# Hybrid retention and attention block: the first value projection as one paired group with seven block products, its heads moved into the second retention iteration

## The reference, cut to what matters

```python
xn = rmsnorm(h, norm_w[l], NORM_EPS)
proj = xn @ w_in[l]
(rq, rk, rv, rz, dq, dk, dv, dz, g_ret, g_diff) = jnp.split(proj, SPLIT_POINTS, axis=-1)
rq = apply_rotary(rq.reshape(b, s, RET_HEADS, RET_QK_DIM), ret_cos, ret_sin)
rk = apply_rotary(rk.reshape(b, s, RET_HEADS, RET_QK_DIM) * (RET_QK_DIM ** -0.5), ret_cos, ret_sin)
o_ret = retention(rq, rk, rv).astype(h.dtype)
o_ret = rmsnorm(o_ret, None, NORM_EPS).reshape(b, s, RET_WIDTH) * jax.nn.silu(rz)
```

## Time and profile before

| what | us |
|---|---|
| three runs | 1080.72, 1080.82, 1082.44 |
| their median | 1080.82 |
| the profiled execution | 1081.12 |
| its span, first to last instruction | 1079.3 |
| PE busy | 1070.8 |
| DVE busy | 801.3 |
| ACT busy | 557.4 |

### The profile page before, as it was taken

How to read it: one execution, slowest core, us unless ns; L and a number is a source line. 1 busy time by engine, 2 the same in 40 slices (tenths; PEclk the granted TensorE clock), 3 DMA queues, 4 the chain that set the end, 5 groups by cost and what they waited for, 6 DMA issues and landing times.

```text
span 1079.3 us, 13314 instructions
## 1 busy us (share of the span) xinstructions
PE 1070.8 (99%) x4840; PEld 891.4 (83%) x4840; DVE 801.3 (74%) x1000; ACT 557.4 (52%) x713; POOL 55.6 (5%) x89
## 2 busy tenths in 40 slices
PE   9999999999999999999999999999999999999997
PEld 7888888888888888888888888888888888888885
DVE  6685576766888978867768686787869875677886
ACT  6554454545646544434644654464465554445554
POOL 0100000000000000000100020010002000111100
PEclk9999999999999999999999999999999999999999
DMA  9887666766665565667576667767766667675763
GB/s 327 303 255 213 192 190 197 242 177 194 184 222 181 193 230 176 211 189 241 166 223 203 205 200 201 237 180 208 209 202 184 217 204 243 234 235 186 263 216 117
DMA packets 122209, 227.98 MB, mean 211 GB/s; under 512 B 14496, under 2 KB 36768, under 8 KB 121632
## 3 DMA queue, kind: packets, MB, share of 16 engines
q1 hardware_dynamic: 120832, 224.76, 66.8%
q0 software_dynamic: 1024, 2.10, 0.5%
q10 hardware_dynamic: 288, 0.27, 0.1%
HBM read 210.84 MB, written 2.10 MB: 197 GB/s over the span
## 4 chain that ended last, share of the span: by engine, by line
PE 97%; DVE 1%; DMA 1%; issue 0%; ACT 0%; DVEq 0%; POOLq 0%; POOL 0%; SPq 0%; ACTq 0%
PE bank L1637 21%; PE bank L1639 21%; PE bank L1638 21%; PE bank L1644 10%; PE bank L1646 10%; PE bank L1645 10%; PE bank L1716 1%; PE bank L1715 1%; PE bank L1714 1%; PE bank L1609 0%; DMA raw<-w_out_dram 0%; PE bank L1613 0%; PE bank L1616 0%; PE bank L1770 0%; PE bank L1730 0%
## 5 line engine op out<-in xcount | busy, mean ns | idle before, releaser
L1145 DVE TENSOR_TENSOR w_lo<-raw,w_hi 128x1024 fp32r<-128x1024 f32 x348 | 426.8, 1236 | 220.9 <-ACT w_hi L798 220.0
L798 ACT ACTIVATE w_hi<-raw 128x1024 fp32r<-128x1024 f32 x348 | 367.0, 1059 | 422.8 <-PE bank L1639 316.1
L1637 PE MATMUL bank<-w_hi,xt_hi 128*128 128x512 f32 x880 | 344.0, 391 | 0.0
L1639 PE MATMUL bank<-w_hi,xt_lo 128*128 128x512 f32 x880 | 342.9, 390 | 0.0
L1638 PE MATMUL bank<-w_lo,xt_hi 128*128 128x512 f32 x880 | 342.8, 390 | 0.0
L1639 PEld LDWEIGHTS bank<-w_hi,xt_lo 128*128 128x128 f32 x880 | 165.3, 188 | 34.6
L1638 PEld LDWEIGHTS bank<-w_lo,xt_hi 128*128 128x128 f32 x880 | 165.4, 188 | 33.7
L1637 PEld LDWEIGHTS bank<-w_hi,xt_hi 128*128 128x128 f32 x880 | 165.3, 188 | 33.6
L1644 PE MATMUL bank<-w_hi,xt_hi 128*128 128x512 f32 x312 | 121.6, 390 | 0.0
L1646 PE MATMUL bank<-w_hi,xt_lo 128*128 128x512 f32 x312 | 121.5, 390 | 0.0
L1645 PE MATMUL bank<-w_lo,xt_hi 128*128 128x512 f32 x312 | 121.5, 389 | 0.0
(11 more groups left out here) (209 smaller groups left out, 1061.3 us busy)
## 6 DMA issues: line engine op xcount, KB each, us to landing
raw<-w_in_dram SPq DMA_DIRECT2D x284, 512.0 KB, 4.3
raw<-w_ret_up_dram SPq DMA_DIRECT2D x32, 512.0 KB, 4.7
raw<-w_diff_up_dram SPq DMA_DIRECT2D x32, 512.0 KB, 4.5
raw<-w_out_dram SPq DMA_DIRECT2D x32, 512.0 KB, 4.5
rot<-squares_t SPq DMA_DIRECT2D x64, 64.0 KB, 2.3
zs<-squares_t SPq DMA_DIRECT2D x48, 64.0 KB, 2.3
normed<-squares_t SPq DMA_DIRECT2D x48, 64.0 KB, 2.2
raw<-w_in_dram SPq DMA_DIRECT2D x8, 256.0 KB, 5.5
```

Source lines behind the costliest of these rows:

```text
L798: act.activation(w_hi[:, s, :, :], raw[:, s, :, :], ACT.Copy).then_inc(hi_ready, 1)
L1145: dve.tensor_tensor(w_lo[:, s, :, :], raw[:, s, :, :], w_hi[:, s, :, :].bitcast(F32), ALU.subtract) \
L1637: pe.matmul(bank[bk][:, :], hi, w_hi[:, s, kk, :], start=k == 0, stop=False)
L1639: return pe.matmul(bank[bk][:, :], lo, w_hi[:, s, kk, :], start=False, stop=k == KT - 1)
```

## The change

The two value groups of the first iteration become a fifth paired phase, `VALUES`, of one group: 16 units of 1024 columns on banks 4 to 7 (own) and 0 to 3 (shared), with seven products at its two places. The values are no longer read from banks but from the joined sums in a row of `gate` (`read_value`, `rest_of_value`), after the group's end. So the first iteration's products of scores by values move from behind units 43 and 50 to behind units 50 and 54, beside the second iteration, and with them everything that follows of these heads. The second iteration's rotation of queries moves from steps 13, 14 to 15, 16. The lambda sums move from step 43 to 38.

```diff
-PAIRED = (U_RET_GATE, U_UP, U_DIFF_GATE, U_OUT)
-PAIRED_FIRST = (G_RET, 0, G_DIFF, 0)
+U_VALUES = U_RET + 4 * UNITS
+PAIRED = (U_VALUES, U_RET_GATE, U_UP, U_DIFF_GATE, U_OUT)
+PAIRED_FIRST = (RV, G_RET, 0, G_DIFF, 0)
...
-SUMS_AT = ((U_RET + RET_UNITS + 34, U_RET + RET_UNITS + 39), (U_RET_GATE + KT + 8, U_RET_GATE + KT + 10),
+SUMS_AT = ((U_RET + 29, U_RET + 31), (U_RET + RET_UNITS + 34, U_RET + RET_UNITS + 39), (U_RET_GATE + KT + 8, U_RET_GATE + KT + 10),
...
-ROTATE_Q, ROTATE_K = 13, 17
+ROTATE_Q, ROTATE_K = (13, 15), 17
+VALUES_AT = ((50, 54), (43, 50))
+HEADS_AT = ((51, 52, 55, 56), (45, 46, 51, 52))
+HEADS_READ_AT = ((54, 55, 60, 61), (49, 50, 56, 57))
+LATE_KEYS_AT = (52, 46)
...
-LAMBDA_AT = U_RET + 43
+LAMBDA_AT = U_RET + 38
...
-    return (lower, upper) if group in (0, 2, 4, 7) else (upper, lower)
+    if group == 0:
+        return (4, 5, 6, 7), (0, 1, 2, 3)
+    return (lower, upper) if group in (1, 3, 5, 8) else (upper, lower)
...
+            def read_value(group, i):
+
+                b, j = pair_blocks(group)[i]
+                act.wait_ge(own_drained, SUMS * group + i + 1)
+                act.activation(v_hi[:, b, j * COLS:(j + 1) * COLS], shared_part(group, i), ACT.Copy, scale=x_rstd[:, b:b + 1]) \
+                   .then_inc(v_hi_ready, 1)
...
-                if s == 40:
+                if it and s == 40:
                     read_v(n0 + 39, 0, 0)
...
+                    if phase == VALUES and s in (KT - 2, KT):
+                        for i in range(SUMS - 1) if s == KT - 2 else (SUMS - 1,):
+                            read_value(group, i)
...
+            def rest_of_value(group, i):
+
+                b, j = pair_blocks(group)[i]
+                cols = slice(j * COLS, (j + 1) * COLS)
+                dve.wait_ge(v_hi_ready, i + 1)
+                dve.scalar_tensor_tensor(out=v_lo[:, b, cols], in0=shared_part(group, i), scalar=x_rstd[:, b:b + 1],
+                                         in1=v_hi[:, b, cols].bitcast(F32), op0=ALU.mult, op1=ALU.subtract).then_inc(values_ready, 1)
...
+                    if phase == VALUES and s in (KT - 1, KT):
+                        for i in range(SUMS - 1) if s == KT - 1 else (SUMS - 1,):
+                            rest_of_value(group, i)
...
-                if s in (43, 50):
-                    for m in range(2 * (s // 50), 2 * (s // 50) + 2):
-                        for b in range(BLOCKS):
-                            pe.wait_ge(drained[2 * (m // 2) + b], ret_low(it, 3))
+                if s in VALUES_AT[it]:
+                    half = VALUES_AT[it].index(s)
+                    for m in range(2 * half, 2 * half + 2):
+                        if it == 0:
+                            pe.wait_ge(values_ready, SUMS)
...
-                for s in range(RET_UNITS):
+                for s in range(RET_UNITS if it else U_VALUES - U_RET):
...
+                if it == 0:
+                    paired_phase(VALUES, xt_hi, xt_lo, xt_lo_ready, KT)
```

More of the change, by code:

```diff
@@ L134, in paired @@
 def paired(n):
-    for phase, first in enumerate(PAIRED):
-        if first <= n < first + PAIR_GROUPS * KT:
-            return phase * PAIR_GROUPS + (n - first) // KT, (n - first) % KT
+    for group in range(LAST_GROUP + 1):
+        if group_start(group) <= n < group_start(group) + KT:
+            return group, n - group_start(group)
     return None, None
@@ L497, in weight_sums @@
         def weight_sums(group):
-            first = (group % PAIR_GROUPS) * PAIR_COLS
-            return (mixed[:, :, PAIR_COLS:], zs[:, :, :], gate[:, :, PAIR_COLS:], mixed[:, :, first:first + PAIR_COLS])[phase_of(group)]
+            first = pair_of(group) * PAIR_COLS
+            return (mixed[:, :, PAIR_COLS:], mixed[:, :, PAIR_COLS:], zs[:, :, :], gate[:, :, PAIR_COLS:], mixed[:, :, first:first + PAIR_COLS])[phase_of(group)]
         def weight_sum(group, i):
@@ L531, in own_full @@
             else:
-                eng.wait_ge(units_done, PAIRED[phase_of(group)] + (group % PAIR_GROUPS + 1) * KT + RING)
+                eng.wait_ge(units_done, group_start(group) + KT + RING)
         def shared_part(group, i):
             cols = slice(i * COLS, (i + 1) * COLS)
+            if phase_of(group) == VALUES:
+                return gate[:, 1, cols]
             if phase_of(group) in (RET_GATE, UP):
@@ L563, in load_unit @@
                     group, k = paired(n)
-                    first = PAIRED_FIRST[phase_of(group)] + (group % PAIR_GROUPS) * PAIR_COLS
+                    first = PAIRED_FIRST[phase_of(group)] + pair_of(group) * PAIR_COLS
                     sp.dma_start(raw[:, s, :, :], w[:, k, first:first + PAIR_COLS].rearrange("p (a c) -> p a c", a=KU)) \
@@ L914, in ret_step @@
                     read_keys_hi(s - 36, scores_t(s - 36), keys_hi(s - 36))
[L915 to L925 removed]
+                if s - LATE_KEYS_AT[it] in (0, 1):
+                    a = s - LATE_KEYS_AT[it]
+                    act.wait_ge(filled[6 + a], ret_high(it, 2) + 1)
+                    read_keys_hi(a, scores_t(2 + a), keys_hi(a))
+                if it and s == 40:
+                    read_v(n0 + 39, 0, 0)
+                if s - 1 in VALUES_AT[it]:
+                    half = VALUES_AT[it].index(s - 1)
+                    for m in range(2 * half, 2 * half + 2):
+                        squares(m, ret_high(it, 2 + half))
+                if s in HEADS_READ_AT[it]:
+                    m = HEADS_READ_AT[it].index(s)
+                    read_ot_hi(m, it * 4 + m, ret_turns(it, 2 + m // 2))
+                if it and s == 48:
                     read_v(n0 + 47, 2, 1)
[L927 to L928 removed]
             def diff_step(it, s):
@@ L1027, in _ @@
                             read_mt_hi(j, half)
[L1028 to L1034, removed]
+                for group in range(LAST_GROUP + 1):
+                    phase, s = phase_of(group), q - group_start(group)
+                    if s == KT - AHEAD:
+                        copy_first(group)
+                    if phase in (RET_GATE, DIFF_GATE) and s == KT:
+                        gates(group)
+                    if phase == VALUES and s in (KT - 2, KT):
+                        for i in range(SUMS - 1) if s == KT - 2 else (SUMS - 1,):
+                            read_value(group, i)
                 if q in (U_OUT - 6, U_OUT - 5):
@@ L1791, in own_free @@
                 own = pair_banks(group)[0]
-                if group == first_group(RET_GATE):
+                if group == first_group(VALUES):
+                    for bk in (0, 1, 6, 7):
+                        pe.wait_ge(drained[bk], ret_low(0, 2) if bk < 2 else ret_high(0, 2))
+                elif group == first_group(RET_GATE):
                     for bk in own[2:]:
@@ L1808, in shared_free @@
                 shared = pair_banks(group)[1]
-                if group in (first_group(RET_GATE), first_group(DIFF_GATE)):
+                if group == first_group(VALUES):
+                    for bk in shared:
+                        pe.wait_ge(drained[bk], ret_low(0, 2))
+                elif group in (first_group(RET_GATE), first_group(DIFF_GATE)):
                     for bk in shared[:2]:
@@ L1850, in paired_phase @@
             def paired_phase(phase, t_hi, t_lo, ready, count):
-                for group in range(first_group(phase), first_group(phase) + PAIR_GROUPS):
+                for group in range(first_group(phase), first_group(phase) + PAIR_PHASE.count(phase)):
                     pair_group(group, t_hi, t_lo, ready, count)
```

126 lines of the change are left out of this document (73 added, 53 removed).

## The result

The change makes the kernel slower: 1087.12 us, the median of six runs (1086.90 to 1088.20), against 1081.09 for the kernel before in the same comparison. The ratio is 1.0056 with a 95% interval of 1.0045 to 1.0067, a loss of 0.56% or 6.0 us. I had predicted 1079.46 us, no measurable difference, with 1081.1 as the upper end.

The account below looks back on a forecast made before the run. The prediction took TensorE's matmuls, 0.2268 us each, to bound the kernel. Six fewer gave -1.36 us, all other terms nothing: 1079.46 us from the 1080.82 median, range 1079.1 to 1081.1.

Parts of the forecast that it names:

- The term of six matmuls: Value stage on PE: 21 matmuls for two units instead of 24, at two places, saving 1.36 us.
- that rival: A left-out matmul gives back less than its distance: six worth 0.79 us, median 1080.03; chance 0.02.
- The three slacks: Value handover, head 3's scores and unit 22's weights: ready 1.0, 0.7 and 1.1 us before PE needs them.
- The rotations: Second iteration, four rotations in a row on DVE: unit 22's remainder ready at 17.98, needed at 19.05; no cost.
- slower by late rotations: DVE enters step 15 late, PE waits for unit 22; two units late gives 1083.8 us; chance 0.07.
- Queues and the rest: SP's later head turns, POOL's unchanged queue order and the earlier lambda sums: all cost nothing.
- Nothing that DVE, ACT or a transfer does is on the path: Long middle of the kernel: PE busy 1029.99 of 1030.00 us, so time is number of matmuls by their distance.

Follow-up runs that it names:

- the run with the other banks: The change, with the second iteration's first z group writing banks 4 and 5 in place of 0 and 1: 1080.31 us, ratio 0.9994.
- the filled wait: The change, with 21 matmuls that nobody reads put on PE before unit 16 of the second iteration: 1085.60 us, ratio 1.0044.
- rotation alone in before: The kernel before, with only the second iteration's query rotation moved from steps 13 and 14 to 15 and 16: 1089.12 us, ratio 1.0077.
- one step later: The change, with the second iteration's query rotation at steps 14 and 15 instead of 15 and 16: 1084.21 us, ratio 1.0028.

## Why the prediction was wrong

**The term of six matmuls was right.** Predicted -1.36 us; the middle without a wait is 137.35 - 135.99 = 1.36 shorter. The 131 ns for a matmul that the Trainium skill states (page "TensorE: Matmul & The Clock Gate", section "Back-to-back issue gap") do not hold here: the six gave back 1.36 us, not the 0.79 estimated from that figure. So that rival falls.

**The three slacks were right.** The last remainder of the values ends at 143.28 + 0.75 = 144.03 and PE asks at 145.21: 1.2, predicted 1.0. Head 3's score remainder ends at 158.06 + 0.55 = 158.61, PE needs it at 158.27 + 1.07 = 159.34: 0.7, as predicted. In the run with the other banks the weights of unit 22 are ready at 199.28 + 1.18 = 200.46 and PE starts that unit at 201.51: 1.05, predicted 1.1. These rows of DVE are, in the change and in that run:

```profile
143.28 0.75 DVE L1236 SCALAR_TENSOR_TENSOR v_lo<-gate,x_rstd,v_hi 128x512 fp32r<-128x512 f32 x1
...
158.06 0.55 DVE L1242 TENSOR_TENSOR ot_lo<-probs,ot_hi 128x384 fp32r<-128x384 f32 x1
```

```profile
199.28 1.18 DVE L1180 TENSOR_TENSOR w_lo<-raw,w_hi 128x1024 fp32r<-128x1024 f32 x1
```

**The step that failed is "The rotations".** There I followed the four rotations only to the next remainder of weights behind them ("Slack 1.1"), that is, to what DVE delivers, and never asked what a rotation gives back. The moved rotation is also the last reader of banks 0 and 1, which PE fills again from unit 16 on. Two rows of the kernel before, which I did not read, hold the answer:

```profile
185.56 0.68 DVE L1177 TENSOR_TENSOR rot<-bank,rope_sb 128x512 f32<-128x512 f32 x1
...
186.76 0.39 PE L1637 MATMUL bank<-w_hi,xt_hi 128*128 128x512 f32 x1
```

Bank 1 is free at 186.24 and PE takes it at 186.76. The margin is 0.52 us, and the diff moves the release two units later, 2 x 2.72 = 5.44, while unit 16 stays. 5.44 - 0.52 = 4.92, and with the 0.10 from the release to PE's start 5.02: the wait measured is 5.01. The length of the wait could have been worked out from the trace of before.

**The rival that came nearest** was slower by late rotations. It had the right rotations, and the wait of its example (4.4, for a DVE two units late) is near the one measured. That nearness is luck. It placed the wait at unit 22, for weights, where the run with the other banks has 1.05 to spare, and not at unit 16, for banks; its condition was that DVE enters step 15 late, which did not happen and got 0.07, while the true wait needs no lateness at all.

**A wait was priced at its length alone.** Even with the wait found, 1080.82 + 5.0 - 1.36 would have given 1084.5. The lower clock behind it costs 2.85 us more, which the filled wait shows apart (2.76). With both, 1080.82 + 6.50 = 1087.3, against 1087.12 measured.

**"Queues and the rest", all at nothing,** held for SP and POOL in the stages that were changed.

**"Nothing that DVE, ACT or a transfer does is on the path"** was read a little too strictly. PE's rows overlap by some 0.17 us (0.39 long, 0.227 apart), so a wait shorter than that shows neither as idle time nor as a wait; only the distance of the starts shows it. The 0.16 before the last group of the kernel before is such a wait, for the load of x.

## What to carry to other kernels

When a step is moved later, list what it releases (banks, buffers) beside what it delivers, and read for each the row of its release and the row of the next user: their distance in the trace of before is all the room there is. On an engine that never waits, any wait is priced at its length and, if it is long enough to lower the clock, at the slow matmuls behind it too. A gain in the middle of a program arrives only if the end isn't held by something else; check what the last stage's transfers have to spare before you count it.

## What the runs showed of the hardware

A wait of PE of 5.0 us was followed by a granted clock of 0.50 over some 5.7 us, at a cost of 2.8 us, in two kernels; behind a wait of 2.3 us the clock stayed at 1.00 in the profiled execution, while the mean clocks of that kernel's ten runs point to a fall in six of them. No run lies between these waits.

The 512 KB load of x took 6.0 to 8.9 us from its issue until ACT began to use it (rotation alone in before: 1029.03 to 1035.05; one step later: 1020.86 to 1029.78), in the seven kernels that issue it at the same unit; ACT then waited for nothing else. What makes it scatter was not tried.
